# Both down projections of two SwiGLU blocks as 2x2 block products in four phases

## What is computed

```python
def _swiglu(h, w_gate, w_up, w_down):
    return (jax.nn.silu(h @ w_gate) * (h @ w_up)) @ w_down

x_new = x_new + g2 * _swiglu(_modulate(x_new, norm_ffn_w[layer], sh2, sc2),
                             w_ffn_gate[layer], w_ffn_up[layer], w_ffn_down[layer])
```

## Time and profile before

| | us |
|---|---|
| median of 3 runs | 3582.68 (3581.99 to 3583.91) |
| profiled execution | 3573.33 |
| its span | 3571.4 |
| PE busy | 3292.8 (92%) |
| DVE busy | 1758.6 (49%) |
| ACT busy | 1189.1 (33%) |
| POOL busy | 550.6 (15%) |
| mean granted TensorE clock | 0.952 |

### The profile page before, as it was taken

One profiled execution on the slowest core, in us unless ns is written; L12 is line 12 of the kernel. 1 busy time (PEld: TensorE's weight loads), 2 busy tenths in 40 slices (PEclk: granted clock), 3 DMA queues, 4 the chain that ended last, 5 costly groups with the idle time before them and its releaser, 6 DMA issues. The chain is left out here.

```text
span 3571.4 us, 38292 instructions
## 1 busy us (share of the span) xinstructions
PE 3292.8 (92%) x15192; PEld 2465.0 (69%) x15192; DVE 1758.6 (49%) x2758; ACT 1189.1 (33%) x1829; POOL 550.6 (15%) x560
## 2 busy tenths in 40 slices
PE   7999998888999999999998988888878899999997
PEld 4476544454778778888886777565456678888886
DVE  6447535546333374444577644345665474443344
ACT  3326523212422153333234232442220253333232
POOL 3100000000100034454001010010000024544000
PEclk8999999996999999999999999998989899999999
DMA  5430010000332232223775123233324132222533
GB/s 229 169 130 13 10 36 13 24 1 1 133 121 89 95 112 83 86 80 115 270 271 212 46 75 91 78 112 123 91 85 154 47 105 87 80 83 97 198 141 118
DMA packets 108921, 366.16 MB, mean 103 GB/s; under 512 B 13991, under 2 KB 31399, under 8 KB 90696
## 3 DMA queue, kind: packets, MB, share of 16 engines
q1 hardware_dynamic: 71032, 244.24, 19.4%
q0 software_dynamic: 21056, 111.05, 8.3%
q10 hardware_dynamic: 16656, 8.42, 1.3%
HBM read 300.63 MB, written 63.05 MB: 102 GB/s over the span
## 5 line engine op out<-in xcount | busy, mean ns | idle before, releaser
L2581 PE MATMUL banks<-hidden_high,down_high 128*128 128x512 f32 x704 | 274.8, 390 | 3.4 <-DVE x L2640 3.4
L2582 PE MATMUL banks<-hidden_low,down_high 128*128 128x512 f32 x704 | 273.9, 389 | 0.0
L2583 PE MATMUL banks<-hidden_high,down_low 128*128 128x512 f32 x704 | 273.9, 389 | 0.0
L1592 PE MATMUL banks<-work,weight_ring 128*128 128x512 f32 (+1 forms) x640 | 264.0, 573 | 0.5 <-ACTq L4305 0.5
L2151 POOL TENSOR_TENSOR quad_raw<-quad_raw 128x512 f32<-128x512 f32 x160 | 230.1, 1439 | 123.4 <-DMA quad_raw<-in_w_gu 117.1
L2283 PE MATMUL banks<-block_t_high,quad_low 128*128 128x512 f32 x608 | 236.5, 389 | 0.0
L2618 DVE TENSOR_TENSOR down_low<-down_raw,down_high 128x2048 fp32r<-128x2048 f32 x44 | 100.9, 2292 | 236.9 <-ACT down_high L2595 236.7
L1592 PEld LDWEIGHTS banks<-work,weight_ring 128*128 128x128 f32 x640 | 126.3, 200 | 129.3 <-issue 123.9
L2595 ACT ACTIVATE down_high<-down_raw 128x2048 fp32r<-128x2048 f32 x44 | 84.3, 1917 | 316.6 <-DMA hidden_raw<-ffn_hidden 316.6
L1774 DVE SCALAR_TENSOR_TENSOR x<-x,work,banks 128x128 f32<-128x128 f32 x320 | 111.3, 348 | 138.1 <-PE banks L1618 127.6
L2281 PE MATMUL banks<-block_t_high,quad_high_b 128*128 128x512 f32 x456 | 177.6, 390 | 0.2 <-ACT quad_partial L2402 0.2
(11 more groups left out here) (607 smaller groups left out, 7458.4 us busy)
## 6 DMA issues: line engine op xcount, KB each, us to landing
down_raw<-in_w_down SPq DMA_DIRECT2D x44, 1024.0 KB, 4.9
quad_raw<-in_w_gu SPq DMA_DIRECT2D x40, 768.0 KB, 4.1
condition_space<-in_mod_w POOLq DMA_DIRECT2D x24, 1024.0 KB, 6.4
ffn_hidden<-quad_gated SPq DMA_DIRECT2D x88, 256.0 KB, 2.0
hidden_raw<-ffn_hidden SPq DMA_DIRECT2D x44, 512.0 KB, 5.9
weight_ring<-in_w_merge SPq DMA_DIRECT2D x24, 512.0 KB, 3.6
quad_raw<-in_w_gu SPq DMA_DIRECT2D x48, 256.0 KB, 3.0
weight_ring<-in_dft SPq DMA_DIRECT2D x12, 1024.0 KB, 5.1
```

The costliest lines, as they stand in the source:

```text
L1592: mm = e.matmul(pg.ps[:, bank_of(h, n), 0:b - a], slot[:, (2 * k + t) * P:(2 * k + t + 1) * P], h1[:, k, a:b], start=(k == 0), stop=(k == ...
L2581: e.matmul(bank, wh[:, k, m], hh[:, k], start=(p == 0 and k == 0), stop=False)
L2582: e.matmul(bank, wh[:, k, m], hl[:, k], start=False, stop=False)
L2583: mm = e.matmul(bank, wl[:, k, m], hh[:, k], start=False, stop=(p == NP - 1 and k == 1))
```

## The change

Write w[k][r] for the weights of hidden tile 2p+k and output tiles 4r to 4r+3, and b[k][s] for hidden tile 2p+k, token half s (in the names of the code b11, b12 are tile 2p's halves, b21, b22 tile 2p+1's). Each pair p of hidden tiles gives a 2x2 by 2x2 block product, formed from seven products in place of eight. The sums are taken over all 11 pairs before they are combined, in four phases (NS is now 39 steps in four slots):

- phase 0, steps 0 to 10: S1 = w[0][0] - w[0][1] and S2 = w[1][1] - S1, made by POOL in the slot, times T3 and T2. S2 is stored to device memory (down_sum).
- phase 1, steps 11 to 21: w[0][0] b11 and w[1][0] b21.
- phase 2, steps 22 to 32: w[1][1] T4 and (w[0][1] + w[1][1]) T1; the sum on POOL.
- phase 3, steps 33 to 38: (w[1][0] - S2) b22, two pairs in a step (the last has one); the difference on POOL.

T1 to T4 are differences of hidden half tiles. DVE makes them for each two tiles at the end of the second (turn_hidden), and SP stores seven half tiles instead of four. Phases 0 to 2 have 24 matmuls a step in 8 banks, phase 3 has 24 in 4 banks (the last step 12).

Between phases ACT copies the eight banks to SBUF (stage_products). POOL combines them (fold, twelve operations at steps 24 to 29), DVE adds the results times the gate onto x (onto, first_products at steps 27 to 30, and at 35, 36, 37 and the end). x comes back in eight DMAs, one behind each of the loads 14 to 21. Conditioning groups lie one to a step at steps 3, 4, 6, 7, 8, 10, 13 to 20, 22 to 26, 31 to 34 and 37, and POOL issues the load of a group behind the weight sums of a step. Squares and their sums move to steps 31, 37, 38 and the end; the matmul with ones stands in front of step 37; the second half's tiles end in the order 4 to 7, 0 to 3. In class Quad the output tiles of even n move to a place of their own (out_tile), with waits that they are turned and stored (out_free); second is cut in two, with the low parts of step 1 between them for the last tile.

```diff
@@ class Quad
+    def out_free(self, e, n, s):
+
+        if n < 2:
+            return
+        if s == 0:
+            self.turned_hidden.wait(e, 4 * (n // 2) if n % 2 else 4 * (n // 2) - 3)
+            self.stored[0].wait(e, 16 * (n - 1))
+        else:
+            self.turned_hidden.wait(e, 4 * (n // 2))
+            self.stored[1].wait(e, 80 * (n // 2))
...
-            for s in range(2):
-                self.out[s].wait(e, n + 1)
-                e.dma_start(self.hidden[n, :, s * HALF:(s + 1) * HALF], self.pg.gated[:, 2 + s, :]).then_inc(self.stored[s].sem, 16)
-
-    def pool(self, e):
+            to = self.hidden[n // 2]
+            self.out[0].wait(e, n + 1)
+            e.dma_start(to[:, BLOCK_21 if n % 2 else BLOCK_11, :], self.out_tile(n, 0)).then_inc(self.stored[0].sem, 16)
+            if n == FT - 1:
+                sum_store(e, 0)
+                down_load(e, 3)
+            if n % 2:
+                self.out[1].wait(e, n + 1)
+                e.dma_start(to[:, BLOCK_22, :], self.out_tile(n, 1)).then_inc(self.stored[1].sem, 16)
+                t1, t2, t4 = self.pg.turned
+                for i, (block, tile) in enumerate(((BLOCK_T1, t1), (BLOCK_T2, t2), (BLOCK_T3, self.pg.even[:, 1, :]), (BLOCK_T4, t4))):
+                    self.turned_hidden.wait(e, 4 * (n // 2) + i + 1)
+                    e.dma_start(to[:, block, :], tile).then_inc(self.stored[1].sem, 16)
...
+        self.stored[1].wait(e, 80 * (n // 2))
+        e.tensor_tensor(t1, b12, b11, ALU.subtract).then_inc(self.turned_hidden.sem, 1)
+        self.turned_hidden.wait(e, at + 1)
+        e.tensor_tensor(t2, b22, t1, ALU.subtract).then_inc(self.turned_hidden.sem, 1)
+        e.tensor_tensor(b12, b22, b12, ALU.subtract).then_inc(self.turned_hidden.sem, 1)
+        self.turned_hidden.wait(e, at + 2)
+        e.tensor_tensor(t4, b21, t2, ALU.subtract).then_inc(self.turned_hidden.sem, 1)
...
+        second_gate(FT - 1)
         down_low(e, 1)
-        second(FT - 1)
+        second_out(FT - 1)
+        self.turn_hidden(e, FT - 1)
@@ def ffn
-        groups_of = {n: (i,) for i, n in enumerate((2, 3, 4, 5, 6, 9, 10, 11))}
-        groups_of.update({n: (8 + 2 * i, 9 + 2 * i) for i, n in enumerate(range(13, 21))})
+        group_of = {n: g for g, n in enumerate((3, 4, 6, 7, 8, 10, *range(13, 21), *range(22, 27), 31, 32, 33, 34, 37))}
...
+                step_done(e, n - SLOTS)
+                if n - SLOTS < NP:
+                    sum_stored[n % 2].wait(e, 16 * ((n - SLOTS) // 2 + 1))
...
+        for n in range(4, NS):
             load(e, n)
-            if n == 7:
-                e.dma_start(x, x_kept).then_inc(x_back.sem, 16)
+            if n - 2 < NP:
+                sum_store(e, n - 2)
+            if 13 < n < 14 + KT:
+                e.dma_start(x[:, n - 14, :], x_kept[:, n - 14, :]).then_inc(x_back.sem, 16)
...
+            if phase == 0:
+                e.tensor_tensor(w[:, 1, :], w[:, 0, :], w[:, 1, :], ALU.subtract).then_inc(sums.sem, 1)
+                sums.wait(e, 2 * n + 1)
+                e.tensor_tensor(w[:, 2, :], w[:, 2, :], w[:, 1, :], ALU.subtract).then_inc(sums.sem, 1)
+            elif phase == 2:
+                e.tensor_tensor(w[:, 0, :], w[:, 0, :], w[:, 1, :], ALU.add).then_inc(sums.sem, 1)
...
+        def condition(e, g):
+            if g >= 2:
+                m_used.wait(e, 2 * (g - 1))
+            e.dma_start(pg.cond_slots[g % 2], m_w[g].rearrange("p (b n) -> p b n", b=2)).then_inc(m_ready[g % 2].sem, 16)
...
+        for n in range(3, NS):
+            weight_sums(e, n)
+            if mod and n in group_of and group_of[n] + 1 < MOD_GROUPS:
+                if group_of[n] == 0:
+                    quad.out[1].wait(e, FT)
+                condition(e, group_of[n] + 1)
+            if 24 <= n < 30:
+                fold(e, 2 * (n - 24))
+                fold(e, 2 * (n - 24) + 1)
...
+            if n in (NP + 1, 2 * NP + 1, PAIRED + 1):
+                stage_products(e, place(n)[0] - 1)
```

More of the change, by code:

```diff
@@ new lines, in ffn, with place, items, loads @@
+    low_tiles, top_tiles = range(KT // 2), range(KT // 2, KT)
+    pg.squares = squares = Squares(pg, [(t, 0) for t in range(KT)] + [(t, 1) for t in (*top_tiles, *low_tiles)])
+    f0 = pg.fill
+    PAIRED = 3 * NP
+    NS = PAIRED + (NP + 1) // 2
+    pg.fill += 2 * KT
+    def place(n):
+        return divmod(n, NP) if n < PAIRED else (3, 2 * (n - PAIRED))
+    def items(n):
+        return min(2, NP - place(n)[1])
+    def loads(n):
+        return 3 * items(n) if n >= PAIRED else (3, 2, 2)[n // NP]
@@ new lines, in turn @@
+    def turn(n):
+        return sum(loads(v) for v in range(n % SLOTS, n + 1, SLOTS))
+    landed = [pg.shared_sem(f"down_loaded_{n}", 16 * sum(loads(v) for v in range(n, NS, SLOTS))) for n in range(SLOTS)]
+    high, low, used = pg.shared_sem("down_high", 2 * NS), pg.shared_sem("down_low", 2 * NS), pg.shared_sem("down_used", NS - 4)
+    sums, part, staged = pg.shared_sem("down_sums", 4 * NP), pg.shared_sem("down_part", 12), pg.shared_sem("down_staged", 24)
+    folded, added = pg.shared_sem("down_folded", 12), pg.shared_sem("down_added", 2)
@@ new lines, in tensor @@
+            low.wait(e, 2 * n + 2)
+            if n == NS - 2:
+                staged.wait(e, 24)
+                squares.roots.sum(e, 0, pg.ps[:, 7, :])
+            for i, (wh, w_low, bh, b_low) in enumerate(products):
+                for m in range(4):
+                    at = m if phase == 3 else 4 * i + m
+                    first = p == 0 and (phase < 3 or i == 0)
+                    end = p + i == NP - 1 if phase == 3 else p == NP - 1
+                    bank = pg.ps[:, at, :]
+                    if n == 0 and at < 6:
+                        last = FT - 2 + at // 3
+                        (quad.silu_1, quad.up_1, quad.gate_2)[at % 3].wait(e, last + (1 if at % 3 == 0 else 1 - DIRECT))
+                    elif first and phase:
+                        staged.wait(e, 8 * (phase - 1) + at + 1)
+                    c = slice(m * P, (m + 1) * P)
+                    e.matmul(bank, wh[:, c], bh, start=first, stop=False)
+                    e.matmul(bank, wh[:, c], b_low, start=False, stop=False)
+                    mm = e.matmul(bank, w_low[:, c], bh, start=False, stop=end)
+                    if end:
+                        mm.then_inc(part.sem if phase == 0 or (phase, i) == (1, 0) else pg.ps_full, 1)
@@ new lines, in onto, with first_products @@
+        def onto(tile, s, product):
+            return e.scalar_tensor_tensor(out=x[:, tile, half(s)], in0=product, scalar=gate(tile), in1=x[:, tile, half(s)],
+                                          op0=ALU.mult, op1=ALU.add)
+        first, second = pg.staged
+        def first_products(q):
+            for i in (2 * q, 2 * q + 1) if q < 2 else ():
+                folded.wait(e, 4 + i + 1)
+                onto(i, 0, second[:, 4 + i, :]).then_inc(pg.ps_free, 1)
+                onto(i, 1, first[:, i, :])
+            for i in (2 * (q - 2), 2 * (q - 2) + 1) if q >= 2 else ():
+                folded.wait(e, 8 + i + 1)
+                onto(4 + i, 0, first[:, 4 + i, :])
+                op = onto(4 + i, 1, first[:, 4 + i, :])
+            if q == 3:
+                op.then_inc(added.sem, 1)
@@ L2638, in evict @@
+        added.wait(e, 2)
+        for i in range(12, 16):
             tile, s = squares.order[i]
             e.wait_ge(pg.ps_full, f0 + i + 1)
[L2640 to L2654 removed]
@@ L2655, in vector @@
-        for i in range(KT, 2 * KT):
-            evict(i)
-            if i >= KT + 2:
+            onto(tile, s, pg.ps[:, i - 12, :]).then_inc(pg.ps_free, 1)
+            if i >= 14:
                 squares.add(e, i - 2)
-        squares.add(e, 2 * KT - 2)
-        squares.add(e, 2 * KT - 1)
+        squares.add(e, 14)
+        squares.add(e, 15)
     pg.stage(name=name, sync=sync, gpsimd=pool, tensor=tensor, scalar=scalar, vector=vector)
```

340 lines of the change are left out of this document (224 added, 116 removed).

## The result

| | before | after |
|---|---|---|
| median | 3584.98 us (10 runs) | 3593.75 us (10 runs) |
| lowest to highest | 3581.99 to 3592.50 | 3588.15 to 3602.69 |
| ratio | | 1.0021, 95% interval 1.0011 to 1.0031 |
| profiled execution, its span | 3573.33, 3571.4 | 3602.69, 3600.5 |
| DVE busy, POOL busy | 1758.6, 550.6 | 2015.3, 763.5 |

The changed kernel takes 0.21% longer by the ratio (some 7.5 us, 4 to 11 by its interval); the two medians differ by 8.8 us. Forecast were 3592 us and +9.6.

A forecast was written before the change was run, and what follows sets the result against it. It took PE to bound both down stages before, and the path shared by DVE and POOL to bind steps 22 to 38 after. First stage +20.9, second -16.3, ends +5: +9.6 us, 3592 us, range 3556 to 3620.

The forecast's parts named there:

- What bounds the kernel, and what is removed: Both down stages: PE-bound; 1056 to 924 matmuls a stage at 0.2267 us, 29.9 us less each, 59.9 for two.
- stretch B of the second stage: Second stage, steps 11 to 21: PE sets the pace, 5.44 us a step without a wait, 60 us.
- The two engines take turns: DVE operations with two SBUF inputs and POOL sums add their times: 105 us against PE's 89.7 in steps 22 to 38.
- rival 2: Clearly faster: DVE's and POOL's work overlaps, PE rules, second stage 210.5 us; -51, total 3532 (3525 to 3562), chance 0.13.
- Rival 1: Shared path costs less; first ground: conditioning reductions don't lock; second: DMAs give 410 GB/s. 3574 us (3562 to 3584), chance 0.27.
- Second stage: 59.8 + 4 for steps 0 to 10, 60 for 11 to 21, 102 for 22 to 38: 226 us against 242.3, -16.3.
- First stage: 74 us for steps 0 to 10, 63 for 11 to 21, 126 for 22 to 38: 263 against 242.1, +20.9.
- the DMA sum: First stage, steps 11 to 21: 24.1 MB take 66 us at 364 GB/s or 59 at 410; taken as 63.
- The ends: End of each stage: squares, root and last evictions crowded into a 2.7 us step; +2.5 us each, +5 (0 to +8).
- The edits costed at nothing: Turned tiles, their waits and stores, ACT's bank copies, x's order: 0 us; if ACT came late, 2 us at three changes.
- The sum: Whole kernel: +20.9 - 16.3 + 5 = +9.6 us, on the before median 3582.7: 3592 us, +0.27%.
- rival 3: Slower: late conditioning groups delay sums through to PE; +9 stretch two, 5 chain, 4 clock; 3610 us (3602 to 3628), chance 0.26.

The follow-up runs named there:

- run 1: Changed kernel with POOL's 56 sums and folds of each down stage cut to 8 of 512 columns: 3552.94 us; first stage 238.1, second 211.6.
- run 2: Changed kernel with each POOL sum and fold replaced by two fills that read nothing: 3552.80 us; first stage 234.8, second 211.4.
- run 10: Changed kernel with 22 of 24 conditioning loads cut to an eighth and the 48 reductions to 8 columns: 3567.20 us; first stage 233.5.
- run 4: Changed kernel with 22 of 24 conditioning loads cut to an eighth of the bytes, reductions whole: 3585.02 us; first stage 253.6.
- run 9: Changed kernel with phase 3's differences made in phase 1, stored and read back, in both stages: 3595.48 us; first stage 261.1, second 223.1.
- run 3: Changed kernel with DVE's 48 conditioning reductions cut to 8 of 1024 columns, loads whole: 3580.61 us; first stage 244.7, second 227.9.
- run 6: Changed kernel with conditioning groups of steps 13 to 20 and 22 to 26 moved to 11 to 18 and 21 to 25: 3594.26 us; first stage 260.2.
- run 5: Changed kernel with x returned as one 4 MiB transfer behind load 14: 3593.59 us; first stage 264.8.
- run 11: Changed kernel with short filler matmuls ahead of PE's long waits: 3590.36 us; first stage 264.3, second 224.2.
- run 7: Change made in the second stage alone, first block as in the kernel before: 3570.92 us, ratio 0.9952; stages 242.5 and 225.4.
- run 8: As run 7, with phase 3's differences made in phase 1, stored and read back: 3565.81 us, ratio 0.9947; second stage 224.0.

## Why the prediction was right

**What bounds the kernel, and what is removed.** Right. Where nothing else is late, the steps take 5.44 us: stretch B of the second stage is 59.9 for a forecast of 60.

**The two engines take turns.** Right, and the step on which all hangs. Runs 1 and 2 take away POOL's reads by themselves, and the second stage goes from 227.3 to 211.5 us; rival 2 had 210.5 for a machine without turns. That the reductions of the conditioning take turns too was open; run 1 shows it. Rival 1's first ground falls with that.

**Second stage.** Forecast 226, measured 227.3: A 63.8 for 63.8, B 59.9 for 60, C and D together 103.6 for 102.

**First stage.** Forecast 263, measured 261.2. A 75.9 for 74 is right by luck: two of its terms were off and cancel. It was to be 7 us over PE's 59.8 by the shared path, 4 for the start and 3 for the row and the first two groups. But most steps of A run at PE's pace (5.4 us); the loss lies in steps 1, 3, 4, 8 and 9. By the runs it is 4 us for the start (A is 63.8 in the second stage), some 7.6 for what run 10 leaves of the groups and the row, and some 4.6 for the groups' work and bytes that run 10 takes away. C and D 120.4 for 126, so 5.6 less than the sum of lock times. That the reductions' mean is 1.52 us, where full turns with a POOL sum would give more, suggests that many of them fell between POOL's sums: adding all lock times comes out too high where one engine waits for data now and then. B 64.9 for 63: the stretch moved 64.9 x 371 GB/s = 24.1 MB, the number of the DMA sum, and its pace at full share was 371/0.97 = 382 GB/s, between the two ends that I had taken (364 and 410). The upper end was misread: 410 is the mean of eleven slices in a row; the eleven fullest average 432, which is 56 us, less than PE needs. Run 4 moves that stretch with the bytes alone, to 59.8. Run 9 moves it to 76.4 with more bytes and eleven POOL sums; where bytes have room, in the second stage, the same edit costs B about 1 us.

**The ends.** The mis-sized term. Forecast +2.5 each; the last square sum of the second stage ends 4.0 us after the last matmul's start, against 4.2 before, so nothing is added there:

```profile
3580.20 0.39 PE L2752 MATMUL banks<-down_last_parts 128*128 128x512 f32 x1
...
3582.68 1.49 DVE L562 TENSOR_TENSOR work<-work 128x512 f32<-128x512 f32 x2
```

In the first stage it is 6.7 us after the last matmul's start at 1969.43, against 4.3. There +2.4 is right in size, but by luck: the conditioning group of step 37 stands on DVE before the last parts and the evictions. DVE, its second reduction and the last square sums:

```profile
1964.11 1.22 DVE L2836 CUSTOM_DVE_ANT_0 condition_row<-condition_space,condition_row 128x1024 f32<-128x1024 f32 x1
...
1973.83 2.28 DVE L562 TENSOR_TENSOR work<-work 128x512 f32<-128x512 f32 x3
```

With the reductions cut to almost nothing (runs 3 and 10) it is 4.7. With the group whole it is 6.7 in runs 6 and 9 as well, but 4.5 and 4.2 in runs 5 and 11, where PE waited longer ahead of step 37 and DVE was ready by the end. So the crowding that I named costs at most 0.5 us, and a group near the end costs 2.0 where PE doesn't come late anyway.

**The edits costed at nothing.** The up/gate stretch ahead of the first stage, from its first matmul to the stage's first, took 428.6 us before and 428.3 after, that of the second 430.4 and 429.9: the turned tiles, their waits and their stores are hidden as said. ACT's copies of banks are not: PE waited 4.1 us for them in the first stage and 2.6 in the second (nearly all at the change to D), where I had named 2 us at each of three changes as the case without cover, and set it at nothing. What failed is the order of ACT's list: the copies stand behind the last parts of step 34, and those waited for POOL's difference. ACT, first stage:

```profile
1929.31 1.06 ACT L2768 ACTIVATE down_last_parts<-down_last 128x1024 fp32r<-128x1024 f32 x1 [4.25 <-POOL down_last L2677]
1930.27 4.00 ACT L2784 ACTIVATE down_staged<-banks 128x512 f32<-128x512 f32 x8
```

That wait is inside C in both stages.

**The sum.** By stretches +19.1 (first), -15.0 (second), +2.4 and -0.2 (ends): +6.3 for a forecast of +9.6; the ratio says +7.5, the medians +8.8. The difference between the sum and the forecast is the ends (2.8) and the spare in C and D, less A, B and the second stage. Between the sum and the total lie 1 to 3 us, which are in code that the diff doesn't touch. The way from the first stage to the second varies by more than that: 1373.5 to 1383.9 us in the runs with the changed first stage, 1374.3 and 1374.6 in runs 7 and 8, 1372.0 before. Whether the change costs anything there is open, so that the total came within 2 us of the forecast is in part luck.

**The clock.** I had it only in rival 3, with 4 us. It costs some 15 us of PE's time in the first stage, but run 11 regains 6 of them and the stage isn't shorter. In C that is explained: DVE's work sets the end there. In A it isn't.

**Rival 3's coupling.** It is there, and small where it can be priced. Ahead of the change to D, POOL waits for a reduction before it asks for a group, and makes the differences of step 34 behind that:

```profile
1926.18 0.58 POOL L2702 DMA_DIRECT2D condition_space<-in_mod_w  x1 [3.32 <-DVE parameters L2836]
```

These are the differences for which ACT waited 4.25 us above. PE's wait at that change is 3.5 us, against 2.6 in the second stage without groups, so the chain costs about 1 us there. POOL waits for reductions 16 times in the first stage, 77.8 us in all; what that costs in C, where DVE is busy all the time, I have not isolated. In A it is not this chain: run 10 waits 5.4 us at step 4 with little left of the groups' work, and there POOL stands 11.9 us for the load of the step itself. That is the term of 3 us for the row and the first two groups, too small.

## What to carry to other kernels

Fewer matmuls pay only until the operands' makers are the limit: add up, stretch by stretch, the DVE operations with two SBUF inputs and POOL's reading operations as one queue, the bytes as another, and compare each with PE. The same edit can win in one place and lose in another; here the block product is worth 15 to 17 us in the stage without conditioning and costs 19 us in the one with it (with the conditioning nearly cut away, run 10, it would be worth 9 there too), so the version that makes the change once is the fast one. Work moved off the shared queue must go to a stretch that has bytes to spare.

## What was not expected of the hardware

- One core moved 391 GB/s over 76 us (run 9, share 1.01), and 371 over 65 us. The Trainium skill names about 358 as a core's HBM limit ("DMA: Bandwidth & Descriptors", Specifications); these stretches, with one core at work, are above it.
- A DVE reduction over 8 columns takes 0.16 us by itself (its shortest rows in run 10) but 0.39 on average beside POOL's sums (runs 3 and 10), and up to 1.25: a short operation can wait for a whole POOL sum all the same.
- A POOL memset of 128x512 takes 0.53 us and stretches no DVE operation (run 2).
- A wait of 5 us is followed by some 5 us of matmuls at half pace, which show as no wait: PE's waits and 924 matmuls at 0.227 us add up to 241.6 us of the first stage's 261.2, and the slower matmuls are some 15 of what is missing.
